# Weight splits moved up at the output product and the side input, side input scaled during the feed-forward, gate's addition to x on VectorE

## What is computed

```python
def layer(x, l):
    y = rms_norm(x, in_norm_g[l]) @ w_in[l] + b_in[l]
    m_out, h_out, s_out = ...
    x = x + concatenate([m_out, h_out, s_out]) @ w_out[l]          # output product
    u = rms_norm(x, mlp_norm_g[l]) @ w_up[l]
    x = x + square(relu(u)) @ w_down[l]                            # feed-forward
    gate = sigmoid(rms_norm(x, ple_norm_g[l]) @ w_ple_gate[l])     # gate
    e = rms_norm(p[l] @ w_ple_proj[l], ple_post_norm_g[l])         # side input
    return x + gate * e
```

## Time and profile before

| | |
|---|---|
| median of 3 runs | 3390.35 us (3390.07 to 3393.16) |
| the profiled execution | 3389.65 us |
| its span, first to last instruction | 3387.8 us |
| PE busy | 3124.5 us, 92% of the span |
| DVE, ACT, POOL busy | 1877.8, 1265.9, 348.1 us |
| mean granted TensorE clock | 0.957 of full |

### The profile page before, as it was taken

The page is one execution under the profiler, slowest core; times in us unless marked ns, Lnnn a source line. Parts: engine busy times, 40 slices in busy tenths (PEclk is TensorE's granted clock), DMA queues, the critical chain, the costliest instruction groups (busy, mean ns, idle before and its releaser), DMA issues.

```text
span 3387.8 us, 37313 instructions
## 1 busy us (share of the span) xinstructions
PE 3124.5 (92%) x14560; PEld 2427.2 (72%) x14560; DVE 1877.8 (55%) x2604; ACT 1265.9 (37%) x2009; POOL 348.1 (10%) x260
## 2 busy tenths in 40 slices
PE   7898899998998899998998997999799889979997
PEld 5677788886677788885666866888656458668886
DVE  6755543467755544466665646444667647464445
ACT  6634322245634322344444333222333423332222
POOL 2000100022000100022001202000210013020001
PEclk9998999999988999999999999999999989989998
DMA  3110233222111222321112312232211113122332
GB/s 133 44 44 32 82 99 97 96 96 72 50 38 41 81 100 94 99 94 61 50 50 82 123 45 69 99 97 96 69 56 56 38 62 131 44 69 95 98 99 76
DMA packets 73723, 259.08 MB, mean 76 GB/s; under 512 B 8020, under 2 KB 10200, under 8 KB 73176
## 3 DMA queue, kind: packets, MB, share of 16 engines
q1 hardware_dynamic: 72824, 252.99, 22.8%
q0 software_dynamic: 736, 3.87, 0.3%
HBM read 254.73 MB, written 2.10 MB: 76 GB/s over the span
## 4 chain that ended last, share of the span: by engine, by line
PE 57%; issue 25%; DVE 10%; ACT 3%; POOLq 2%; DVEq 1%; DMA 0%; ACTq 0%; POOL 0%
PE bank L496 42%; DVE w_lo L1759 3%; POOLq L2531 2%; PE bank L987 2%; PE bank L998 1%; ACT w_hi L1154 1%; PE bank L704 1%; PE bank L557 1%; PE bank L1008 1%; PE bank L545 1%; PE bank L1012 1%; PE bank L1024 1%; PE bank L743 1%; PE bank L766 1%; PE bank L731 1%
## 5 line engine op out<-in xcount | busy, mean ns | idle before, releaser
L496 PE MATMUL bank<-a_hi,w_hi 128*128 128x512 f32 x2040 | 829.7, 407 | 96.0 <-DVE a_lo L1789 46.3
L496 PE MATMUL bank<-a_hi,w_lo 128*128 128x512 f32 x2040 | 803.6, 394 | 0.0
L496 PE MATMUL bank<-a_lo,w_hi 128*128 128x512 f32 x2040 | 803.1, 394 | 0.0
L1759 DVE TENSOR_TENSOR w_lo<-w_raw,w_hi 128x1024 fp32r<-128x1024 f32 (+1 forms) x474 | 632.3, 1335 | 280.9 <-ACT w_hi L1154 279.7
L496 PE MATMUL bank<-b_hi,w_hi 128*128 128x512 f32 (+1 forms) x1688 | 646.5, 383 | 49.0 <-DVE w_lo L1759 21.0
L1154 ACT ACTIVATE w_hi<-w_raw 128x1024 fp32r<-128x1024 f32 (+1 forms) x474 | 494.3, 1044 | 419.0 <-DMA w_raw<-weights 418.8
L496 PE MATMUL bank<-b_lo,w_hi 128*128 128x512 f32 (+1 forms) x1688 | 636.9, 377 | 0.0
L496 PE MATMUL bank<-b_hi,w_lo 128*128 128x512 f32 (+1 forms) x1688 | 636.2, 377 | 0.0
L496 PEld LDWEIGHTS bank<-a_hi,w_hi 128*128 128x128 f32 x2040 | 388.8, 191 | 209.8 <-issue 67.1
L496 PEld LDWEIGHTS bank<-a_lo,w_hi 128*128 128x128 f32 x2040 | 389.5, 191 | 85.9 <-issue 7.9
L496 PEld LDWEIGHTS bank<-a_hi,w_lo 128*128 128x128 f32 x2040 | 388.4, 190 | 83.8
(11 more groups left out here) (280 smaller groups left out, 3040.7 us busy)
## 6 DMA issues: line engine op xcount, KB each, us to landing
w_raw<-weights SPq DMA_DIRECT2D x458, 512.0 KB, 3.4
w_raw<-weights SPq DMA_DIRECT2D x16, 384.0 KB, 2.9
x<-x SPq DMA_DIRECT2D x8, 256.0 KB, 7.2
mem<-mem POOLq DMA_DIRECT2D x2, 1024.0 KB, 5.0
out<-x SPq DMA_DIRECT2D x8, 256.0 KB, 2.0
mem<-mem SPq DMA_DIRECT2D x1, 1024.0 KB, 12.0
ple<-ple POOLq DMA_DIRECT2D x2, 512.0 KB, 3.8
o<-c_level SPq DMA_DIRECT2D x1, 512.0 KB
```

The costliest lines, as they stand in the source:

```text
L496: last = mm(bank[G_BANK[u % 4] if at is None else at][:, 0:cols], w[:, u % SLOTS, ks], t[:, k, 0:cols], start=(k == 0 and n == 0), stop=(k ...
L1759: tt(w_lo[:, u % SLOTS, w], w_raw[:, u % SLOTS, w], f32(w_hi[:, u % SLOTS, w]), ALU.subtract).then_inc(w_lo_ready, 1)
```

## The change

In `mix1` the PE pair takes its banks by the usual rotation, ACT and DVE split two more units (first+25, first+26) before the window attention. In `ffn1` PE waits for all eight side tiles before its third unit and not only before the sum of squares. In `proj` ACT and DVE split up to three units ahead at the start and after each half, and ACT takes the root after the second square. The scaling of the side tiles moves from the gate to the down part of the first feed-forward chunk. In the gate DVE makes e * y and then adds it to x; POOL no longer adds there.

```diff
--- before.py
+++ after.py
@@ -331,7 +331,7 @@
         p_hi_ready, p_ready, e_made, e_taken = sem("p_hi_ready"), sem("p_ready"), sem("e_made"), sem("e_taken")
         met = {n: sem(f"met_{n}") for n in ("pe", "act", "dve", "pool")}
 
-        e_gated, y_scaled = sem("e_gated"), sem("y_scaled")
+        y_scaled = sem("y_scaled")
         t_made, conv_made, g_qk, gates_split, gates_log, gates_made, g_end = (
             sem("t_made"), sem("conv_made"), sem("g_qk"), sem("gates_split"), sem("gates_log"), sem("gates_made"), sem("g_end"))
         g_cols, g_ends, g_copied, g_gate, g_valued, g_v, g_ones = (
@@ -794,7 +794,7 @@
                                               s_prob_t[l][:, half_, q, 2 * e + i, :], start=(i == 0), stop=(i == len(back) - 1))
                         last.then_inc(a_out, 1)
 
-                pair(a, a_ready, at=(bank_in(first, first), bank_in(first, first + 1)))
+                pair(a, a_ready)
                 sum_squares()
                 halves_of(2)
                 if l == 0:
@@ -913,8 +913,8 @@
                     if first:
                         pe.wait_ge(e_taken, 8 * l + 4)
                         pair(a, a_ready)
+                        pe.wait_ge(e_taken, 8 * (l + 1))
                         unit(a)
-                        pe.wait_ge(e_taken, 8 * (l + 1))
                         sum_squares()
                     for j in range(3 if first else 0, 8):
                         unit(a)
@@ -1504,8 +1504,10 @@
                 level_take(8)
                 ahead(first + 24)
                 finish(20)
+                ahead(first + 25)
                 finish(21)
                 finish(22)
+                ahead(first + 26)
                 act.wait_ge(h_summed, l + 1)
                 for p in range(2):
                     f(o[:, 2 + p, :], bank[6 + p][:, :], ACT.Copy).then_inc(h_out, 1)
@@ -1541,14 +1543,15 @@
                     step(lambda u: round_x(a, k, col("mlp_g", l, k)))
 
             def proj(l):
-                for part in range(2):
-                    for j in range(4):
-                        k = 4 * part + j
-                        act.wait_ge(e_taken, 8 * l + k + 1)
-                        square(y[:, 8 + k, :])
-                    step()
-                    if part == 0:
+                ahead(c.unit + 3)
+                for k in range(8):
+                    act.wait_ge(e_taken, 8 * l + k + 1)
+                    square(y[:, 8 + k, :])
+                    if k == 1:
                         root_of_mean()
+                    if k in (3, 7):
+                        c.unit += 1
+                        ahead(c.unit + 3)
 
             def ffn1(l):
                 a, h = operands(1, l)
@@ -2211,6 +2216,7 @@
 
             def proj(l):
                 base = c.unit
+                ahead(base + 3)
                 for part in range(2):
                     for j in range(4):
                         if j < 3:
@@ -2220,9 +2226,8 @@
                         b = 5 + j if part == 1 and j < 3 else G_BANK[(base + j) % 4 if part == 0 else base % 4]
                         dve.tensor_copy(y[:, 8 + 4 * part + j, :], bank[b][:, :]).then_inc(e_taken, 1)
                     dve.drain().then_inc(bank_free, 1)
-                    if c.next < c.unit + SLOTS:
-                        split_lo()
                     c.unit += 1
+                    ahead(c.unit + 3)
                 recip(r_x)
 
             def ffn1(l):
@@ -2239,6 +2244,9 @@
                             recip(r_post)
                     for k in range(8):
                         step(add_to_x(k, (a, col("ple_g", l, k)) if last else None))
+                        if first:
+                            e = y[:, 8 + k, :]
+                            stt(e, e, col("post_g", l, k), r_post[:, :], ALU.mult, ALU.mult)
 
                 ahead(c.unit + 3)
                 chunk(first=True)
@@ -2253,10 +2261,10 @@
 
                 def combine(k):
                     e = y[:, 8 + k, :]
-                    stt(e, e, col("post_g", l, k), r_post[:, :], ALU.mult, ALU.mult)
+                    dve.wait_ge(act_made, c.since(act_made, k + 1))
+                    tt(e, e, y[:, k, :], ALU.mult)
                     dve.drain()
-                    dve.wait_ge(act_made, c.since(act_made, k + 1))
-                    tt(e, e, y[:, k, :], ALU.mult).then_inc(e_gated, 1)
+                    tt(x[:, k, :], x[:, k, :], e, ALU.add).then_inc(x_ready, 1)
 
                 ahead(c.unit + 3)
                 recip(r_x)
@@ -2601,7 +2609,7 @@
                 out1(l)
                 add_squares()
                 add_squares()
-                add_squares(before=lambda k: ahead(k, e_gated, 8))
+                add_squares()
 
             pool.wait_ge(x_ready, DT * 3 * LAYERS)
             pool.dma_start(dil[:, :], dram["c_dilated"]).then_inc(dil_landed, 16)
```

## The result

The changed kernel takes 3341.22 us (median of 4 runs, 3335.91 to 3350.45) against 3390.21 (4 runs, 3389.91 to 3393.16): the ratio is 0.9857, 95% interval 0.9845 to 0.9869. It is faster by 49 us, and the forecast was 3340.0. The profiled execution took 3335.91 us with a span of 3334.1, 53.7 less than before. Of all executions of the study one stands apart: one of the four of experiment 2 took 4018.3 us at a mean granted clock of 0.734, against 3343.81 to 3345.27 us at 0.962 for its other three, and no trace of it was kept.

A forecast was written before the change was run, and what follows sets the result against it. PE bounds the kernel (busy 92%), so only its stalls and half-clock stretches can be won. 13.2 - 1.6 + 22.0 - 1.0 + 9.0 + 8.0 = 49.6 us off 3389.65 gives 3340.0 us; range 3333 to 3350.

The forecast's parts named there:

- All six stalls: PE's stalls in output product, before feed-forward and behind gate, both layers; each costs its length plus half the slow stretch.
- The end of the mixer: Price of the two early splits before `level_sums`: 0.8 us per layer taken, bounds 0 and 2.8.
- the lower row: End of mixer: the split before the fifth `rope_sin`, not meeting POOL, takes 1.22 us and makes it 0.6 us late.
- The arrears of DVE in the feed-forward: DVE starts the feed-forward 2 to 3 us behind; 0.5 us per layer allowed, bounds 0 and 2.
- the rival of the first chunk: DVE's arrears reach PE in the first feed-forward chunk, 2 to 3 us per layer; 3346 us, chance 0.12.
- The clock rival: Granted clock falls to half in the longer feed-forward without pause; one layer's late part gives 3415 us; chance 0.02.
- The rival of the side input's splits: Early split waits for its landing and delays the copies; half of 22 us stays, 3351 us, chance 0.05.
- The side input: Its early splits remove PE's stall before the feed-forward: 8.9 us plus 2.05 slow stretch, 11.0 per layer.
- The gate: DVE's step in the gate falls from 6.18 to 4.3 to 5.4 us, so PE's 5.44 sets the pace.
- the 2 us per end of the rival: Gate stays at DVE's pace, last low part 2 us late; two ends give 12, not 17 us; 3345, chance 0.15.
- Gate to the next mixer: Layer 0: `pair` no longer waits for the eighth tile's bank; 9.0 us taken, bounds 6.5 and 9.5.
- The two ends together: Gate ends: 9.0 us to the next mixer in layer 0 plus 8.0 to `fused` in layer 1, 17 us.

The follow-up runs named there:

- experiment 2: Changed kernel with POOL adding to x in the gate again, scaling still in the feed-forward; 3344.71 us.
- experiment 5: Changed kernel without the two splits before the window attention, on ACT and DVE; 3344.11 us.
- experiment 6: Changed kernel with the side input of before on ACT and DVE (one split behind each half, root after the fourth square); 3351.28 us.
- experiment 11: Kernel before with only the mixer's two splits moved up, on ACT and DVE; 3360.65 us.
- experiment 12: Changed kernel with POOL's sums of the gate only one of 512 columns wide (result wrong); 3346.40 us in its only run.
- experiment 1: Changed kernel with the gate as before: side tiles scaled in the gate, POOL adding to x; splits stay moved; 3359.52 us.
- experiment 4: Changed kernel with the mixer's pair given its banks again, so it waits for the gate's last tile; 3336.16 us.
- experiment 3: Changed kernel with the scaling back in the gate, the add to x staying on DVE; 3343.77 us.
- experiment 7: Changed kernel with the first of the mixer's two splits behind the fifth `rope_sin` on DVE; 3334.68 us.
- experiment 10: Changed kernel with that first split behind the fifth `rope_sin`, and `fused`'s third unit not waiting for DVE's take; 3322.58 us.

## Why the prediction was right, and where its steps were not

**The stalls and their price.** All six stalls went, and the pricing (the length of the stall, and half of the slow stretch behind it) held to the tenth: 6.6 forecast for the output product, 6.60 measured; 11.0 for the side input, 11.00 and 11.04. No stall above 1 us opened in their place.

**The end of the mixer.** Forecast 0.8 per layer, measured 0.42. The split in front of the fifth `rope_sin` met no POOL instruction (1.22 us), and its uncovered part was even less than the 0.6 of the lower row:

```profile
243.67 1.22 DVE L1762 TENSOR_TENSOR w_lo<-w_raw,w_hi 128x1024 fp32r<-128x1024 f32 x1
244.80 0.69 DVE L2054 TENSOR_TENSOR o<-bank,sin_t 128x512 f32<-128x512 f32 x1
```

```profile
245.64 0.62 PE L723 MATMUL bank<-h_d,v 128*64 128x128 f32 x7 [1.30 <-DVE o L2054]
```

PE's wait for `rope_sin` rose from 0.88 to 1.30. The second split hid in DVE's idle time, as said.

**The arrears of DVE in the feed-forward.** Allowed 0.5 per layer, measured 0: the stage took 343.62 us in every profile, so neither the rival of the first chunk nor a cost of the moved scaling shows. DVE's side input after:

```profile
352.04 2.80 DVE L1762 TENSOR_TENSOR w_lo<-w_raw,w_hi 128x1024 fp32r<-128x1024 f32 x2 [0.72 <-ACT w_hi L1154]
354.75 2.48 DVE L2227 COPY y<-bank 128x512 f32<-128x512 f32 x4
359.95 2.28 DVE L1762 TENSOR_TENSOR w_lo<-w_raw,w_hi 128x1024 fp32r<-128x1024 f32 x1 [2.72 <-ACT w_hi L1154]
362.15 2.47 DVE L2227 COPY y<-bank 128x512 f32<-128x512 f32 x4
368.03 2.28 DVE L1762 TENSOR_TENSOR w_lo<-w_raw,w_hi 128x1024 fp32r<-128x1024 f32 x1 [3.41 <-ACT w_hi L1154]
370.24 3.34 DVE L1786 RECIPROCAL r_x<-root 128x512 f32<-128x512 f32 x1
373.69 0.69 DVE L2239 SCALAR_TENSOR_TENSOR y<-bank,r_x 128x512 f32<-128x512 f32 x1
```

The first take at 373.69 lies 2.7 us behind the end of the pair's first unit, as forecast; the margin was enough. The clock rival didn't come true in the profile: the 343 us from 377 on ran at 1.00 without a pause. The rival of the side input's splits didn't either: they lie ahead of the copies, at 352.04.

**The side input: right sum, but not its only cause.** I wrote that the side input's own early splits remove the 9 us. They do so alone (experiment 5, 22.20), but experiments 6 and 11 show that they aren't needed for most of it: with the mixer's two splits alone the stage takes 23.26, and the side input's edit then adds only 1.1 us per layer. My step counted how early a split stands in its own stage, and overlooked that a unit gained at the end of the mixer is carried by every `step` behind it: in the side input the split behind the first half is then already the one that the pair needs.

**The gate.** Steps of 4.3 to 5.4 us were forecast, with PE setting the pace; measured 4.13 to 5.32 while DVE caught up, then 5.44. The eighth tile is taken at 754.30, 0.2 us behind PE's last matmul of the gate, as forecast (771.1 for 770.92). One step and two late low parts, to be held against the earlier trace rows:

```profile
743.91 0.68 DVE L2273 TENSOR_TENSOR y<-bank,r_x 128x512 f32<-128x512 f32 x1
744.51 0.68 DVE L2265 TENSOR_TENSOR y<-y 128x512 f32<-128x512 f32 x1
745.26 0.69 DVE L2267 TENSOR_TENSOR x<-x,y 128x512 f32<-128x512 f32 x1
746.24 1.23 DVE L1762 TENSOR_TENSOR w_lo<-w_raw,w_hi 128x1024 fp32r<-128x1024 f32 x1 [0.28 <-ACT w_hi L1154]
747.38 0.75 DVE L1792 SCALAR_TENSOR_TENSOR b_lo<-x,vec,b_hi 128x512 fp32r<-128x512 f32 x1
748.86 0.69 DVE L2273 TENSOR_TENSOR y<-bank,r_x 128x512 f32<-128x512 f32 x1 [0.74 <-PE bank L496]
...
757.79 1.87 DVE L1792 SCALAR_TENSOR_TENSOR b_lo<-x,vec,b_hi 128x512 fp32r<-128x512 f32 x1
...
760.95 1.79 DVE L1792 SCALAR_TENSOR_TENSOR b_lo<-x,vec,b_hi 128x512 fp32r<-128x512 f32 x1
```

The scaling is gone, the split takes 1.23 us instead of 2.23, the low part 0.75 where it comes before POOL's sum and 1.87 where it comes behind it. POOL's side of it, against the earlier trace rows:

```profile
747.42 1.86 POOL L2538 TENSOR_TENSOR sq_sum<-sq_sum,sq 128x512 f32<-128x512 f32 x1 [3.98 <-ACT sq L1187]
...
757.82 1.29 POOL L2538 TENSOR_TENSOR sq_sum<-sq_sum,sq 128x512 f32<-128x512 f32 x1 [3.58 <-ACT sq L1187]
```

At 747.42 POOL waits for the low part that began at 747.38 (1.86 us); at 757.82 it goes first, takes 1.29, and the low part 1.87. The row of that low part starts 0.03 us before POOL's, but the split ahead of it ends only at 757.88, when POOL was already waiting. In experiment 12, with POOL's sums one column wide, every low part takes 0.75. That is the rule of the Trainium skill, "SBUF — State Buffer", "Who interferes with whom": a DVE instruction with two SBUF inputs and a GpSimd instruction reading SBUF exclude one another for a whole instruction. The traces agree: 205 times in the profile after, and 224 times in that of before, a 128x512 sum of POOL's and a DVE instruction with two SBUF inputs overlap, and never are both at their short length; beside a DVE instruction that reads a bank, POOL's sum has its short length 52 times in the profile after. It cost 1.0 us in layer 0 (45.43 against 44.42): the last low part ends 10.3 us behind the gate, where PE wants it 9.5 behind. That is why this end gave 8.53 and not the 9.5 of its upper bound, of which 9.0 was taken; it isn't the 2 us per end of the rival.

**Gate to the next mixer.** I put the 7.7 us down to `pair` waiting for the last bank, which was late. Only the lateness counts. With the gate as it was, taking the wait away leaves 53.36 of 53.96 (experiment 1), and with the new gate it is worth 0.1 us (experiment 4), while the gate's own edits with the wait already gone are worth 7.9. `fused`, which kept its wait, gained as much, 8.47 where 8.0 was forecast. The two ends together came out at the 17.0 of the sum, but by luck: one is 0.5 below its term, the other 0.5 above.

**The total.** The terms as measured sum to 51.4, against 49.6 forecast; the difference is the price at the end of the mixer (0.85 instead of 1.6) and the arrears (0 instead of 1.0). That the median came out within 1.3 us of the forecast is luck: the kernel's single runs lie between 3335.9 and 3350.5 us, its median was 3343.36 the second time, and the profiled run gained 53.7.

## What to carry to other kernels

When each stage does "its own work, then one split", the distance by which splits run ahead is a state handed from stage to stage: look for the place where it is lost, and buy it back in the last stretch where the engines wait anyway, before adding splits at the stall itself. A bank wait that ends a stall may only stand in for an engine that is late; shorten that engine's step first and then see what the wait is worth. When two engines exclude one another, count both engines' instructions in one line to find the length of a step.

## What the runs showed of the hardware

The changed kernel's runs spread over 14.6 us (nine runs, 3335.87 to 3350.45), those before over 10.9 us (3385.25 to 3396.19), and the longer runs have the lower mean granted clock (0.963 to 0.958, and 0.958 to 0.954). The window attention at the end of the mixer is where it shows. Windows from `level_sums` to the output product, the two layers of the profile after and then layer 1 of experiment 1:

```profile
245.60:305.20 59.60, 52.02 (x408) 40.68 (x408) 33.52 (x128) 32.58 (x95) 1.14 (x2) 0.80 0.01 1
969.80:1032.40 62.60, 55.38 (x409) 42.84 (x409) 33.63 (x128) 32.57 (x95) 1.50 (x3) 0.73 0.01 2
```

```profile
983.40:1052.80 69.40, 61.94 (x409) 48.57 (x409) 33.63 (x128) 32.50 (x95) 1.53 (x3) 0.66 0.01 1
```

PE has the same 408 or 409 matmuls, DVE and ACT are busy for the same 33.6 and 32.5 us, but the clock is 0.80, 0.73 and 0.66 of full, and the stretch takes 59.6, 62.6 and 69.4 us. In the other profiles of the study it was 59.6 or 62.6 in most layers, 62.9 in layer 1 of the kernel before, 64.5 once (experiment 2) and 69.3 twice more (experiments 3 and 12); only the 63.6 of experiments 7 and 10 goes with an edit. So some 10 us can hang on where the clock's low stretches fall in a chain of small matmuls. Why they fall as they do is open; no run here tried it.
